# Scores of two heads at a time in the first block's attention of a fused two-block kernel

## The chip, the cores and the metric

The kernel runs on one core of one Trainium2 chip. The metric is the device time of one execution in microseconds, the median of the runs. The core has five engines with a queue of instructions each: TensorE (PE in the profile), VectorE (DVE), ScalarE (ACT), GpSimd (POOL) and SyncE (SP, which issues the transfers). Each takes its queue in order, and they wait for each other through semaphores.

## What is computed

Two transformer-like blocks are applied to 256 tokens of width 1024. The change is in the first block's attention, which has three kinds with eight heads each, 64 wide: `slc` (causal over selected blocks; with 256 tokens and 64-token blocks all of them are selected), `win` (a causal window) and `dsa` (each query sees the 64 keys that an indexer scores highest). Cut to what matters:

```python
# per kind and head; tq = query position, kpos = key position
s = jnp.einsum('bqd,bkd->bqk', q, k) * HEAD_DIM ** -0.5
p = masked_softmax(s, mask)          # mask: kpos <= tq; for dsa also "among the top 64"
o = jnp.einsum('bqk,bkd->bqd', p, v)
# slc and win: head h uses key/value group h // 4; dsa: one key and value for all heads
```

Beside it `mod = c @ w_ada + b_ada` is needed, a row of 6144 numbers from a 1024 x 6144 matrix.

## The kernel before, in words

All of it is one program with a hand-written order on every engine. The weights come through a ring of four 1 MB tiles in SBUF, loaded by SyncE in a fixed order.

The attention of the first block is a loop over 24 units, `UNITS1` (L243): `slc` heads 0 to 7, `win` heads 0 to 7, `dsa` heads 0 to 7. I call the steps of unit i as follows, with the line that the profile gives:

- S(i), PE, `scores` (L752, matmuls by the helper at L659): for each of the two blocks of 128 queries one fp32 matmul of the query (64 x 128) with the keys (64 x 128, then 64 x 256), and behind each a bf16 matmul of an identity (128 x 128) with the mask, which adds the mask in PSUM. Queries and keys of a head lie on half of the partitions: of group `h // 4` (`slc`, `win`) or `h % 2` (`dsa`). The result is 128 x 384 in PSUM bank i % 2.
- M(i), DVE, L2013: two row maxima of that bank.
- E(i), ACT, L1349: two exponentials out of the bank into `prob`, with row sums. Its end frees the bank.
- T(i), PE, `turn` (L764, matmuls at L768): three 128 x 128 transposes of `prob` into bank 2 + i % 2.
- C(i), DVE, L2021: the copy of that bank to SBUF.
- V(i), PE, `values` (L772, L659 again): three fp32 matmuls (128 x 128 with 128 x 64) into the banks of the kind's output.

PE's queue holds in turn S(i), T(i-1), V(i-2) (L789 to L795). DVE's queue (`attention` at L2004) holds in turn M(i), C(i-1) and then `after1(i - 2)` (L2034), which carries work from beside the attention:

- K, `key_round` (L1960, L1967 to L1976): one of 16 rounds that find the top 64 keys for `dsa`, 8 for each block of queries. The last of a block writes the mask `maskd`, which S of the first `dsa` unit waits for.
- W, `weigh` (L1819, L1829 and L1831): one of 16 tiles of `w_ada`, four DVE instructions of 128 x 512 that add up columns times `c`. It stands in every second step up to unit 13 and in every step after that.
- O, `weighted` and `coefficients` (L1978, L1993): twice, for `slc` and for `win`, the output of a finished kind is scaled and added.

The PSUM banks are planned by `attention_groups` (L247). Behind the attention PE runs `modulation(1)` (L738), 64 matmuls with one moving column, and then the output projection.

Of the kernel before, what the change touches and what calls it, by code (L numbers as in the profile page):

```python
# [28 lines left out]
TB = T // P  # L29
# [3 lines left out]
HEADS = 8  # L33
# [10 lines left out]
DSA_K = min(256, T // 4)  # L44
# [195 lines left out]

UNITS1 = [(kind, h) for kind in ("slc", "win", "dsa") for h in range(HEADS)]  # L243
O_BANK = {"slc": 4, "win": 6, "dsa": 4}


def attention_groups(group, units):  # L247
    n = len(units)
    for i in range(n + 2):
        if i < n:  # L250
            group(("S", *units[i]), i % 2)
        if 1 <= i <= n:
            group(("PT", *units[i - 1]), 2 + (i - 1) % 2)
        if i >= 2 and units[i - 2][1] == 0:
            for tb in range(TB):
                group(("O", units[i - 2][0], tb), O_BANK[units[i - 2][0]] + tb)


IN2_KIND = ["mq"] + [name for name in ("hgf", "hgq", "sbq", "sbk", "hig", "sbv") for _ in range(2)]
# [21 lines left out]
def build(nc, x_in, mem_in, pos_in, vec_in, ident_in, const_in, w_in, out):  # L281
    with ExitStack() as ctx:
# [60 lines left out]
        identb = take(P // 2).bitcast(BF16)  # L343
# [295 lines left out]
        def _(pe):  # L639
            order = iter(PLAN)  # L640

            def begin(name):

                assert next(order) == name, name
                bank, use = PLAN[name]
                if use > 1:
                    pe.wait_ge(drained[bank], use - 1)
                return banks[bank]

            def end(ins, name):  # L650
                ins.then_inc(full[PLAN[name][0]], 1)
# [4 lines left out]
                    pe.wait_ge(loaded[n % RING], 16 * (n // RING + 1))  # L656

            def mm(out_, lhsT, rhs, start=True, stop=True):
                return nc.tensor.matmul(out_, lhsT, rhs, start=start, stop=stop)  # L659

            def both_halves(ps, cols, head):

# [85 lines left out]
            def attention(units, operands, v_of, cols, mask):  # L748

                n = len(units)  # L750

                def scores(i):  # L752
                    ps = begin(("S", *units[i]))
                    for tb in range(TB):
                        q, k = operands(units[i], tb)
                        a, b = cols[tb]
                        m = mask(units[i], tb)
                        last = mm(ps[:, a:b], q, k, stop=(m is None))
                        if m is not None:
                            lo, mat = m  # L760
                            last = mm(ps[:, a + lo:b], identb, mat, start=False)
                    end(last, ("S", *units[i]))

                def turn(i):  # L764
                    wait_read(pe, ("S", *units[i]))
                    ps = begin(("PT", *units[i]))
                    for c in range(cols[1][1] // P):
                        last = nc.tensor.transpose(ps[:, c * P:(c + 1) * P],  # L768
                                                   prob[:, i % 2, c * P:(c + 1) * P], ident[:, :])
                    end(last, ("PT", *units[i]))  # L770

                def values(i):  # L772
                    kind, h = units[i]
                    if h == 0:
                        for tb in range(TB):
                            begin(("O", kind, tb))
                    wait_read(pe, ("PT", kind, h))
                    for tb in range(TB):
                        ps = banks[PLAN[("O", kind, tb)][0]]
                        a, b = cols[tb]  # L780
                        for c in range(a // P, b // P):
                            last = mm(ps[:, h * HD:(h + 1) * HD], probT[:, i % 2, c * P:(c + 1) * P],
                                      v_of(units[i], c - a // P), start=(c == a // P), stop=(c == b // P - 1))
                        if i + 1 == n or units[i + 1][0] != kind:
                            end(last, ("O", kind, tb))
                    pe.drain().then_inc(s_pvd, 1)

                base = 0 if units is UNITS1 else len(UNITS1)
                for i in range(n + 2):  # L789
                    if i < n:  # L790
                        scores(i)
                    if 1 <= i <= n:
                        turn(i - 1)
                    if i >= 2:
                        values(i - 2)  # L795


            pe.wait_ge(s_small, SMALL)
# [5 lines left out]
            out_ = [begin(("mkv", tb)) for tb in range(TB)]  # L804
            for half in range(2):
                arrived(("mem_kv", 0, half))
                for tb in range(TB):
                    for kk in range(4):
                        k = 4 * half + kk
                        last = mm(out_[tb][:, :], hT[:, k, tokens(tb)], km(("mem_kv", 0, half))[:, kk, :],  # L810
                                  start=(k == 0), stop=(k == KD - 1))
# [9 lines left out]
            ps = begin(("mkT",))  # L821
            for pr in range(2):
                for tb in range(TB):
                    last = nc.tensor.transpose(ps[:, pr * T + tb * P:pr * T + (tb + 1) * P],
                                               mkv[:, tb, pr * P:(pr + 1) * P], ident[:, :])
            end(last, ("mkT",))
            pe.wait_ge(s_rot, 1)
            for n in range(7):
                ps = begin(("pairT", n))
                for s in range(2):  # L830
                    pair = 2 * n + s
                    for tb in range(TB):
                        cols = slice(s * T + tb * P, s * T + (tb + 1) * P)
                        if pair < PAIR_KD:
                            first = 2 * pair if pair < PAIR_KS else 2 * pair + 2
                            last = nc.tensor.transpose(ps[:, cols], rot[:, tb, first * HD:(first + 2) * HD],
                                                       ident[:, :])
                        else:
                            r = ROT_KD if pair == PAIR_KD else ROT_KI
                            last = both_halves(ps, cols, rot[:, tb, r * HD:(r + 1) * HD])  # L840
# [3 lines left out]
            for which, src, first in (("kcT", rot, ROT_KC * HD), ("vcT", plain, PL_VC)):  # L844
                ps = begin((which,))
                for g in range(2):
                    for tb in range(TB):
                        a = first + g * HD
                        last = both_halves(ps, slice(g * T + tb * P, g * T + (tb + 1) * P), src[:, tb, a:a + HD])
                end(last, (which,))  # L850
            for which in range(2):
# [3 lines left out]
                ps = begin(("cmp", which))  # L855
                for m in range(16):
                    last = mm(ps[:, 0:45], w1[:, m, :], kvT[which][:, :, 2 * m:2 * m + 225:16],
                              start=(m == 0), stop=(m == 15))
# [3 lines left out]
            ps = begin(("kcmp",))  # L862
            for g in range(2):
                last = mm(ps[g * HD:(g + 1) * HD, 0:N_CMP], vall("w2k"), hidk[:, g, 0:N_CMP])
            end(last, ("kcmp",))
            wait_read(pe, ("cmp", 1))
            ps = begin(("vblk",))
# [5 lines left out]
            for g in range(2):  # L873
                ps = begin(("Sc", g))
                rows = slice(g * HD, (g + 1) * HD)
                for tb in range(TB):
                    for r in range(4):
                        c = (tb * 4 + r) * 16
                        last = mm(ps[:, c:c + N_CMP], pairT[rows, PAIR_QN + r, tokens(tb)], kcmpT[rows, 0:N_CMP])
                end(last, ("Sc", g))  # L880

            for n in range(4):
                tb, odd = n // 2, n % 2
                width = (tb + 1) * P
                ps = begin(("L", n))
                rows = slice(odd * HD, (odd + 1) * HD)
                for i in range(2):
                    last = mm(ps[:, i * width:(i + 1) * width], pairT[rows, PAIR_QI + i, tokens(tb)],
                              pairT[rows, PAIR_KI, 0:width])
                end(last, ("L", n))  # L890
            pe.wait_ge(s_pcz, 1)
            ps = begin(("pcT",))
            for tb in range(TB):
                last = nc.tensor.transpose(ps[:, tb * P:(tb + 1) * P],
                                           sc[:, tb * HEADS:(tb + 1) * HEADS, :].rearrange("p h n -> p (h n)"),
                                           ident[:, :])
# [3 lines left out]
            for tb in range(TB):  # L900
                ps = begin(("Oc", tb))
# [32 lines left out]
            for n in range(4):  # L934
                ps = begin(("gg", n))
                for k in range(4):
                    last = mm(ps[:, k * P:(k + 1) * P],
                              gg[:, 4 * n + k:4 * n + k + 1].to_broadcast([P, P]), ident[:, :])
# [5 lines left out]
            out_ = {}  # L944
# [766 lines left out]
        def _(dve):  # L1711
# [248 lines left out]
            def key_round(i):  # L1960


                tb, r = i // 8, i % 8
                width = (tb + 1) * P
                s, w = score[:, tb, 0:width], work[:, tb, 0:width]
                if r == 0:
                    link(tt(score[:, tb, tb * P:width], score[:, tb, tb * P:width], con("causal"), ALU.add))  # L1967
                src = s if r == 0 else w
                link(nc.vector.max(cmax[:, 0:8], src))
                link(nc.vector.match_replace(w, cmax[:, 0:8], src, TAKEN))  # L1970
                if r == DSA_K // 8 - 1:

                    link(ts(w, w, 0.5 * TAKEN, NEG, ALU.is_ge, ALU.mult))
                    if tb:
                        nc.vector.tensor_copy(maskd[:, tb, 0:P], w[:, 0:P])
                    tt(maskd[:, tb, tb * P:width], w[:, tb * P:width], con("causal"), ALU.add).then_inc(s_maskd, 1)  # L1976
# [56 lines left out]

            def after1(i):  # L2034

                if 0 <= i + 2 < TB * DSA_K // 8:
                    key_round(i + 2)
                if i + 2 >= 16 or i % 2 == 0:
                    if rest:
                        weigh(rest.pop(0))  # L2040
                if i in (8, 16):
                    kind = UNITS1[i - 1][0]
                    coefficients(kind, 1 if kind == "slc" else 2)
                    for tb in range(TB):
                        weighted(kind, ("O", kind, tb), tb, 0, True)
# [472 lines left out]
```

## Time and profile before

| | us |
|---|---|
| median of 3 runs | 1652.7 |
| lowest and highest run | 1650.15, 1653.73 |
| time of the profiled execution | 1652.53 |
| its span in the trace | 1650.7 |
| PE busy, PEld (weight loads) busy | 1497.5, 1307.3 |
| DVE busy | 968.1 |
| ACT busy | 725.8 |
| POOL busy | 1005.4 |

PE's busy time is modelled where matmuls overlap, so 91% busy isn't 91% used. The table is a sum over stages that differ; the attention above is 107 us of the span, and the page's row of PE's clock shows which of the two levels (half or full) was granted in each slice. The chain of work that ended last, cut to a stretch, tells there which engine the others waited for; gaps in an engine's own line tell what it waited for.

### The profile page before, as it was taken

How to read it: one execution, taken by the hardware profiler on the slowest of the kernel's cores; microseconds unless marked ns; L12 is line 12 of the kernel's file. 1: busy time of each engine (PE TensorE's matmuls, PEld its weight loads, DVE VectorE, ACT ScalarE, POOL GpSimd, SP SyncE). 2: the span in 40 equal slices, each digit the busy share in tenths (PEclk: the TensorE clock that was granted, in tenths of full speed). 3: DMA queues.
4: the chain of work that ended last, by engine and by line, in shares of the span. 5: the costliest groups of instructions: out<-in, count | busy, mean ns of one | idle time of the engine just before them, and what ended most of it. 6: DMA issues, size and time to landing. Idle time of an engine off the chain costs nothing.

```text
span 1650.7 us, 24575 instructions
## 1 busy us (share of the span) xinstructions
PE 1497.5 (91%) x9944; PEld 1307.3 (79%) x9944; DVE 968.1 (59%) x1618; ACT 725.8 (44%) x1292; POOL 1005.4 (61%) x729
## 2 busy tenths in 40 slices
PE   0699899969999599979998989999999999999998
PEld 0378567759987588658998989999998878888886
DVE  4463788255511586452586583877768999952221
ACT  2234211355644566434444545334343444445554
POOL 0162000337676354135699899666667878889997
PEclk9998555789999799989999999999999999999999
DMA  6444235225555232124544445433433443445552
GB/s 264 171 153 154 77 128 204 76 78 179 179 179 185 96 128 103 52 76 149 187 175 169 167 169 187 137 145 132 151 129 130 151 150 134 152 172 185 200 183 102
DMA packets 34481, 244.99 MB, mean 148 GB/s; under 512 B 3904, under 2 KB 4288, under 8 KB 5184
## 3 DMA queue, kind: packets, MB, share of 16 engines
q1 hardware_dynamic: 33376, 241.19, 41.0%
q10 hardware_dynamic: 992, 2.23, 0.4%
q8 instruction: 79, 1.29, 0.3%
q14 instruction: 34, 0.28, 0.0%
HBM read 242.36 MB, written 1.05 MB: 147 GB/s over the span
## 4 chain that ended last, share of the span: by engine, by line
PE 76%; DVE 12%; ACT 3%; POOL 3%; issue 2%; PEld 2%; DMA 1%; PEldq 0%; ACTq 0%; DVEq 0%
PE bank L659 34%; PE bank L1236 20%; PE bank L691 20%; POOL v_lo L1706 2%; PEld bank L691 2%; DVE ada L1831 2%; PE bank L1020 1%; DMA arena<-pos_dram 1%; DVE arena L1831 1%; DVE hot L2375 1%; ACT arena L1294 1%; POOL v_lo L1696 1%; DVE arena L2256 1%; DVE x L1798 1%; PE bank L768 0%
## 5 line engine op out<-in xcount | busy, mean ns | idle before, releaser
L1706 POOL TENSOR_TENSOR v_lo<-ring,v_hi 128x512 fp32r<-128x512 f32 x512 | 712.5, 1407 | 136.0 <-ACT v_hi L1650 120.5
L1696 POOL TENSOR_TENSOR v_lo<-ring,d_hi 128x512 fp32r<-128x512 f32 x213 | 292.8, 1384 | 499.8 <-ACT d_hi L1336 436.0
L1650 ACT CAST v_hi<-ring 128x512 fp32r<-128x512 f32 x512 | 317.9, 622 | 452.5 <-PE bank L659 238.7
L659 PE MATMUL bank<-hT_hi,v_hi 128*128 128x256 f32 x1024 | 293.2, 286 | 8.7 <-POOL v_lo L1706 8.7
L659 PE MATMUL bank<-hT_lo,v_hi 128*128 128x256 f32 x1024 | 288.3, 282 | 0.0
L659 PE MATMUL bank<-hT_hi,v_lo 128*128 128x256 f32 x1024 | 286.9, 280 | 0.0
L1336 ACT CAST d_hi<-ring 128x512 fp32r<-128x512 f32 x236 | 143.5, 620 | 174.9 <-PE bank L691 140.1
L1236 PE MATMUL bank<-v_hi,mix_hi 128*128 128x512 f32 x512 | 206.9, 404 | 0.4 <-DVE mix_lo L2392 0.4
L659 PEld LDWEIGHTS bank<-hT_hi,v_hi 128*128 128x128 f32 x1024 | 194.6, 190 | 10.1 <-POOL v_lo L1706 8.2
L1236 PE MATMUL bank<-v_hi,mix_lo 128*128 128x512 f32 x512 | 201.0, 392 | 0.0
L1236 PE MATMUL bank<-v_lo,mix_hi 128*128 128x512 f32 x512 | 199.8, 390 | 0.0
L659 PEld LDWEIGHTS bank<-hT_lo,v_hi 128*128 128x128 f32 x1024 | 193.3, 189 | 0.0
L659 PEld LDWEIGHTS bank<-hT_hi,v_lo 128*128 128x128 f32 x1024 | 192.4, 188 | 0.0
L1781 DVE TENSOR_TENSOR v_lo<-ring,d_hi 128x512 fp32r<-128x512 f32 x71 | 62.8, 885 | 219.0 <-ACT d_hi L1336 210.8
L2392 DVE TENSOR_TENSOR mix_lo<-arena,mix_hi 128x512 fp32r<-128x512 f32 x64 | 86.7, 1355 | 133.0 <-ACT mix_hi L1662 133.0
L659 PE MATMUL bank<-arena 128*128 128x128 f32 (+7 forms) x600 | 145.1, 391 | 13.2 <-DVE arena L2185 3.1
L691 PE MATMUL bank<-hT_hi,d_hi 128*128 128x256 f32 x528 | 149.3, 283 | 5.9 <-issue 2.9
L691 PE MATMUL bank<-hT_lo,d_hi 128*128 128x256 f32 x528 | 148.5, 281 | 0.0
L691 PE MATMUL bank<-hT_hi,v_lo 128*128 128x256 f32 x528 | 147.7, 280 | 0.0
L659 PEld LDWEIGHTS bank<-arena 128*128 128x128 f32 (+3 forms) x600 | 105.8, 250 | 48.9 <-issue 35.6
L659 PE MATMUL bank<-hotg,hot 128*128 128x64 bf16 x1536 | 116.8, 241 | 4.0 <-DVE mix_lo L2392 2.6
L659 PEld LDWEIGHTS bank<-hotg,hot 128*128 128x128 bf16 x1536 | 94.0, 119 | 25.0 <-issue 11.8
(308 smaller groups left out, 2547.8 us busy)
## 6 DMA issues: line engine op xcount, KB each, us to landing
ring<-w_dram SPq DMA_DIRECT2D x228, 1024.0 KB, 4.8
arena<-mem_dram ACTq DMA_DIRECT2D x1, 1024.0 KB, 8.4
x<-x_dram SPq DMA_DIRECT2D x1, 1024.0 KB, 7.5
out_dram<-x SPq DMA_DIRECT2D x1, 1024.0 KB, 4.0
arena<-const_dram ACTq DMA_DIRECT2D x1, 884.0 KB, 18.4
arena<-vec_dram ACTq DMA_DIRECT2D x1, 144.0 KB, 15.3
ident<-ident_dram ACTq DMA_DIRECT2D x1, 64.0 KB, 10.6
iota<-ident_dram ACTq DMA_DIRECT2D x1, 64.0 KB, 12.8
```

What stands on the lines that cost most here:

```text
L659: return nc.tensor.matmul(out_, lhsT, rhs, start=start, stop=stop)
L691: last = nc.tensor.matmul(out_, l, m, start=start and part == 0, stop=stop and part == 2, skip_group_check=True)
L1020: return nc.tensor.matmul(out_, lhsT, rhs, start=start, stop=stop, skip_group_check=True)
L1236: last = nc.tensor.matmul(acc[tb, c][:, :], w[:, q % 2, t], v[:, r, :], start=False, stop=(q == PAIRS - 1 and jj == 1 and part == 2), skip ...
L1294: link(nc.scalar.activation(junk, src[:, tb, :], ACT.Square, accum_out=ssq[:, 2 * i + tb:2 * i + tb + 1]))
L1336: nc.scalar.copy(d_hi[:, r, :], dense_quarter(d, r)).then_inc(s_dhi, 1)
L1650: nc.scalar.copy(v_hi[:, r, :], quarter(at, r)).then_inc(s_vhi, 1)
L1696: nc.gpsimd.tensor_tensor(v_lo[:, r, :], dense_quarter(d, r), d_hi[:, r, :], ALU.subtract).then_inc(s_dpl, 1)
L1706: nc.gpsimd.tensor_tensor(v_lo[:, r, :], quarter(at, r), v_hi[:, r, :], ALU.subtract).then_inc(s_plo if r < 3 else w_used, 1)
L1781: tt(v_lo[:, 3, :], dense_quarter(d, 3), d_hi[:, 3, :], ALU.subtract).then_inc(s_dvl, 1)
L1831: ins = stt(acc, w, vcol("c", k), acc, ALU.mult, ALU.add)
L2392: tt(mix_lo[:, q % 2, :], pair_weights(q), mix_hi[:, q % 2, :], ALU.subtract).then_inc(s_mlo, 1)
```

## The change

The units are put in the order of heads 0, 4, 1, 5, 2, 6, 3, 7 for `slc` and `win`, so that two neighbours lie on different halves of the partitions; `dsa` heads have that already. PE takes two units in a step: S of both units, with the four mask matmuls first and then the score matmuls of the two heads in turn; then T, V, T, V. Before the pair of S it waits until both banks are free. DVE's and ACT's loops stay, but for the key rounds, which come one step earlier.

```diff
-UNITS1 = [(kind, h) for kind in ("slc", "win", "dsa") for h in range(HEADS)]
+PAIRED = {"slc": (0, 4, 1, 5, 2, 6, 3, 7), "win": (0, 4, 1, 5, 2, 6, 3, 7), "dsa": range(HEADS)}
+UNITS1 = [(kind, h) for kind in ("slc", "win", "dsa") for h in PAIRED[kind]]
...
             def mm(out_, lhsT, rhs, start=True, stop=True):
-                return nc.tensor.matmul(out_, lhsT, rhs, start=start, stop=stop)
+                return nc.tensor.matmul(out_, lhsT, rhs, start=start, stop=stop, skip_group_check=True)
...
                 def scores(i):
-                    ps = begin(("S", *units[i]))
+                    two = [begin(("S", *units[i + j])) for j in range(2)]
                     for tb in range(TB):
-                        q, k = operands(units[i], tb)
                         a, b = cols[tb]
-                        m = mask(units[i], tb)
-                        last = mm(ps[:, a:b], q, k, stop=(m is None))
-                        if m is not None:
-                            lo, mat = m
-                            last = mm(ps[:, a + lo:b], identb, mat, start=False)
-                    end(last, ("S", *units[i]))
+                        m = [mask(units[i + j], tb) for j in range(2)]
+                        for j in range(2):
+                            lo, mat = m[j]
+                            mm(two[j][:, a + lo:b], identb, mat, start=(tb == 0), stop=False)
+                    for tb in range(TB):
+                        a, b = cols[tb]
+                        for j in range(2):
+                            q, k = operands(units[i + j], tb)
+                            last = mm(two[j][:, a:b], q, k, start=False, stop=True)
+                            if tb == TB - 1:
+                                end(last, ("S", *units[i + j]))
...
-                for i in range(n + 2):
+                for i in range(0, n + 4, 2):
                     if i < n:
                         scores(i)
-                    if 1 <= i <= n:
-                        turn(i - 1)
-                    if i >= 2:
-                        values(i - 2)
+                    for j in (i - 2, i - 1):
+                        if 0 <= j < n:
+                            turn(j)
+                        if 0 <= j - 1 < n:
+                            values(j - 1)
...
             def after1(i):
 
-                if 0 <= i + 2 < TB * DSA_K // 8:
-                    key_round(i + 2)
+                if i + 2 == 0:
+                    key_round(0)
+                if i + 3 < TB * DSA_K // 8:
+                    key_round(i + 3)
```

`attention_groups` (the plan of the banks) follows PE's new order, with the same banks.

On PE, in the middle of the `slc` units, there stood before (bank0 and bank1 hold scores, bank2 and bank3 transposes, bank4 and bank5 outputs; "drained" is the semaphore that a bank's reader raises) V, S of one unit and the T of the unit before it:

```order
L659 MATMUL bank4<-arena 128x64 [waits bank3_drained]
L659 MATMUL bank5<-arena 128x64 x2
L659 MATMUL bank0<-arena 128x128 [waits bank0_drained]
L659 MATMUL bank0<-arena 128x128
L659 MATMUL bank0<-arena 128x256
L659 MATMUL bank0<-arena 128x128
L768 MATMUL bank3<-ident,arena 128x128 [waits bank3_drained,bank1_drained]
L768 MATMUL bank3<-ident,arena 128x128 x2
```

and now the same place reads:

```order
L666 MATMUL bank0<-arena 128x128 [waits bank1_drained,bank0_drained]
L666 MATMUL bank1<-arena 128x128
L666 MATMUL bank0<-arena 128x128
L666 MATMUL bank1<-arena 128x128
L666 MATMUL bank0<-arena 128x128
L666 MATMUL bank1<-arena 128x128
L666 MATMUL bank0<-arena 128x256
L666 MATMUL bank1<-arena 128x256
L779 MATMUL bank2<-ident,arena 128x128 [waits bank2_drained,bank0_drained]
L779 MATMUL bank2<-ident,arena 128x128 x2
L666 MATMUL bank4<-arena 128x64 [waits bank3_drained]
L666 MATMUL bank5<-arena 128x64 x2
```

The first transpose of the older pair (into bank2) now stands behind the scores of the younger pair, and these wait for both score banks.

On DVE the place of the loop is this, now, in the `dsa` units (the maxima of an odd unit, the copy of the even unit before it, W, the maxima and the copy of the next step, W):

```order
L2024 TENSOR_REDUCE stat<-bank 128x1 [waits bank1_drained,bank1_full,w_used]
L2024 TENSOR_REDUCE stat<-bank 128x1
L2032 COPY arena<-bank 128x384 [waits unit_done,bank2_full]
L1842 SCALAR_TENSOR_TENSOR arena<-ring,arena 128x512 [waits slot3_loaded]
L1842 SCALAR_TENSOR_TENSOR arena<-ring,arena 128x512 [waits vector_step] x3
L2024 TENSOR_REDUCE stat<-bank 128x1 [waits bank0_drained,bank0_full,w_used]
L2024 TENSOR_REDUCE stat<-bank 128x1
L2032 COPY arena<-bank 128x384 [waits unit_done,bank3_full]
```

This order of maxima, copy and W is the one of before; nothing stands between the maxima of the odd unit (bank1) and the copy from bank2.

## Rows read from the trace of the kernel before

**Rows 1.** Page, the span in 40 slices of 41.3 us, tenths
```profile
PE   0699899969999599979998989999999999999998
DVE  4463788255511586452586583877768999952221
PEclk9998555789999799989999999999999999999999
```
**Rows 2.** Busy time by stretch: PE, PEld, DVE, ACT, POOL, then granted clock, DMA
```profile
178.00:216.00 38.00, 35.39 (x129) 25.17 (x129) 30.80 (x80) 8.21 (x36) 0.00 (x0) 0.53 0.31 111
216.00:256.00 40.00, 36.28 (x126) 25.55 (x125) 33.28 (x76) 8.22 (x36) 0.00 (x0) 0.50 0.37 132
256.00:285.00 29.00, 26.40 (x97) 19.82 (x96) 27.35 (x50) 5.48 (x24) 0.00 (x0) 0.50 0.62 218
```
**Rows 3.** Chain that ended last, slc units: start us, us, what
```profile
188.74 0.64 PE bank L768 x3
189.38 1.17 PE bank L659 x6
190.55 0.08 issue
190.63 2.38 PE bank L659 x6
193.01 0.64 PE bank L768 x3
```
**Rows 4.** The same chain, dsa units and behind the attention
```profile
268.24 0.41 DVE stat L2013
268.65 0.46 DVE arena L2021
...
272.12 0.41 DVE stat L2013
...
284.69 1.54 PE bank L659 x6
286.24 0.26 issue
286.49 13.80 PE bank L659 x64
```
**Rows 5.** Groups of DVE, 178 to 285 us: busy, mean ns, idle before
```profile
L2021 DVE COPY arena<-bank 128x384 f32<-128x384 f32 x24 | 13.3, 552 | 0.4 <-PE bank L768 0.3
L2013 DVE TENSOR_REDUCE stat<-bank 128x1 f32<-128x128 f32 x24 | 7.0, 292 | 12.4 <-issue 7.2 <-PE bank L659 4.7
```
**Rows 6.** Timeline of all engines, 171 to 200 us
```profile
178.06 0.62 DVE L2013 TENSOR_REDUCE stat<-bank 128x1 f32<-128x128 f32 x2 [1.01 <-PE bank L659]
...
183.95 0.20 ACT L1349 ACTIVATION_READ_ACCUMULATOR arena<-bank,stat 128x1 f32 x1
...
184.20 0.90 PE L768 MATMUL bank<-ident,arena 128*128 128x128 f32 x3 [1.59 <-ACT arena L1349]
...
185.14 0.56 DVE L2021 COPY arena<-bank 128x384 f32<-128x384 f32 x1 [0.29 <-PE bank L768]
...
193.10 0.62 DVE L2013 TENSOR_REDUCE stat<-bank 128x1 f32<-128x128 f32 x2 [1.95 <-issue]
...
193.81 0.37 ACT L1349 ACTIVATE arena<-bank,stat 128x128 f32<-128x128 f32 x1 [2.71 <-PE bank L659]
...
194.52 0.20 ACT L1349 ACTIVATION_READ_ACCUMULATOR arena<-bank,stat 128x1 f32 x1
```
**Rows 7.** Timeline of PE's weight loads inside one S, then T
```profile
190.62 0.50 PEld L659 LDWEIGHTS bank<-arena 64*128 64x128 f32 x2 [0.26 <-issue]
191.35 0.72 PEld L659 LDWEIGHTS bank<-arena 128*128 128x128 bf16 x3 [0.22 <-issue]
192.72 0.10 PEld L659 LDWEIGHTS bank<-arena 128*128 128x128 bf16 x1 [0.65 <-issue]
```
**Rows 8.** Indexer scores: timeline of PE; matmuls of L659 at 165.70 to 165.80
```profile
164.04 3.16 PE L659 MATMUL bank<-arena 64*128 64x128 f32 x15
L659 PE MATMUL bank<-arena x4: 631/631/631, 165.3 to 165.7; 64*128 64x256 f32 x4
```

More of the change, by code:

```diff
@@ L248, in attention_groups, with first @@
     n = len(units)
-    for i in range(n + 2):
-        if i < n:
-            group(("S", *units[i]), i % 2)
-        if 1 <= i <= n:
[L253 to L256, printed above, removed]
+    def first(i):
+        if 0 <= i < n and units[i][1] == 0:
+            for tb in range(TB):
+                group(("O", units[i][0], tb), O_BANK[units[i][0]] + tb)
+    for i in range(0, n + 4, 2):
+        if i < n:
+            group(("S", *units[i]), 0)
+            group(("S", *units[i + 1]), 1)
+        for j in (i - 2, i - 1):
+            if 0 <= j < n:
+                group(("PT", *units[j]), 2 + j % 2)
+            first(j - 1)
 IN2_KIND = ["mq"] + [name for name in ("hgf", "hgq", "sbq", "sbk", "hig", "sbv") for _ in range(2)]
@@ L752, in scores @@
                 def scores(i):
-                    ps = begin(("S", *units[i]))
+                    two = [begin(("S", *units[i + j])) for j in range(2)]
                     for tb in range(TB):
-                        q, k = operands(units[i], tb)
                         a, b = cols[tb]
-                        m = mask(units[i], tb)
-                        last = mm(ps[:, a:b], q, k, stop=(m is None))
-                        if m is not None:
-                            lo, mat = m
-                            last = mm(ps[:, a + lo:b], identb, mat, start=False)
-                    end(last, ("S", *units[i]))
+                        m = [mask(units[i + j], tb) for j in range(2)]
+                        for j in range(2):
+                            lo, mat = m[j]
+                            mm(two[j][:, a + lo:b], identb, mat, start=(tb == 0), stop=False)
+                    for tb in range(TB):
+                        a, b = cols[tb]
[4 more added lines that the diff above has]
+                                end(last, ("S", *units[i + j]))
                 def turn(i):
@@ L786, in values @@
                     pe.drain().then_inc(s_pvd, 1)
-                base = 0 if units is UNITS1 else len(UNITS1)
-                for i in range(n + 2):
+                for i in range(0, n + 4, 2):
                     if i < n:
                         scores(i)
-                    if 1 <= i <= n:
-                        turn(i - 1)
-                    if i >= 2:
-                        values(i - 2)
+                    for j in (i - 2, i - 1):
+                        if 0 <= j < n:
+                            turn(j)
+                        if 0 <= j - 1 < n:
+                            values(j - 1)
             pe.wait_ge(s_small, SMALL)
```

## The prediction

> **What bounds the kernel now.** I began with the page's slices [rows 1]: PE is nearly full everywhere, but in slices 4 to 6 (165 to 289 us), where the attention lies, the granted clock is 5 tenths, the 1.2 GHz level. So this stage runs at half speed although PE looks busy. The busy time by stretch [rows 2] splits it by kind: in the `slc` units DVE is busy 30.8 of 38 us, in the `win` units 33.3 of 40, in the `dsa` units 27.4 of 29, and PE 35.4, 36.3 and 26.4. Two engines are close to each other, so the chain must say which one the others wait for. In the `slc` units it runs on PE alone [rows 3]: T 0.64, V 1.17, issue 0.08, S 2.38, a period of 4.27 us (188.74 to 193.01). In the `dsa` units it runs on DVE [rows 4]: maxima, copy, W, 3.88 us from 268.24 to 272.12; with the other form of W 4.14. The `win` units lie between. Behind the last V stand 13.80 us of one-column matmuls on PE [rows 4], which nothing in the change touches.
>
> What DVE loses in the whole stage stands before its maxima and copies: 7.2 + 4.7 + 0.3 = 12.2 us [rows 5], of which the first 1.0 comes before the first unit [rows 6]. So **11.2 us are DVE's waits inside the stage**, out of the 106.6 from the first maxima (178.06) to the last copy (284.6); the other 95.4 are work that it does one piece after the other and that the change only reorders. No version in which DVE does the same work can gain more than those 11.2 us.
>
> **The change, part by part.**
>
> *Scores.* Today one S is 0.08 + 2.38 = 2.46 us. In it are four score passes (each fp32 matmul of L659 is two), of 128, 128, 256 and 256 columns, and two masks. A pass of 128 columns costs 0.21 us where nothing disturbs it (T is three in 0.64 [rows 3]), so four passes would be 6 x 0.213 = 1.28 us and two masks at most as much as two transposes, 0.43. The rest, some 0.75 us or more, is lost at the changes between 64 rows and 128 rows: from the first score load to the first mask load 0.73 us pass (190.62 to 191.35) for two passes worth 0.43 [rows 7], and there are four such changes in a unit. The new pair has two in all.
>
> Do the two halves run side by side? The trace has such a case: the indexer's scores, whose last two groups lie on different halves. 15 passes, eight of 256 and six of 128 columns and a short one, take 3.16 us from the first start to the modelled end of the last [rows 8]; end to end they would need 22 x 0.213 = 4.7. And four matmuls of 256 columns, 0.43 us each, start between 165.3 and 165.7 [rows 8]. So they overlap. For the pair I have 0.45 for four masks (a mask's load is 0.10 us [rows 7]; between 0.10 and 0.21 each), 0.3 for two changes, 1.35 for the scores (1.28 if wholly side by side, 2.56 if not at all) and 0.1 for the first load: **2.2 us for two units instead of 4.9**. The bounds are 2.0 and, if nothing at all is won, 4.9.
>
> The overlap works across the order of issue here, since matmuls of the second half start before the last of the first half. The Trainium skill, "TensorE: Matmul & The Clock Gate", section "The mechanism", says otherwise: matmuls start and end strictly in the order of the program, and only weight loads of another row group are pulled ahead. This is the third rival below.
>
> *PE's demand* falls by that from 8.54 to 2 x (0.64 + 1.17) + 2.2 = 5.8 us for a pair. PE isn't the bound any more in any kind. If that were all, DVE would bound the stage.
>
> *The order of the waits.* It isn't all. The pair of S waits for both score banks, so for E of both units of the pair before, and T of the even unit stands behind it on PE. DVE's queue has M(i+1), C(i) with nothing between, and C(i) needs T(i). So after M(i+1), i even, DVE stands still while the whole chain runs: from the end of the maxima to E 0.09 (193.10 + 0.62 to 193.81), E 0.91 (to 194.52 + 0.20), to PE 0.05 (184.15 to 184.20), the pair of S 2.2, and from the start of T to C 0.94 (184.20 to 185.14) [rows 6]. **Together 4.19 us, once for each pair.** None of it is hidden: K, W and the next maxima are all queued behind C(i) on DVE, and ACT and PE have nothing left of the older pair. Before, C(i-1) needed T(i-1), for which PE had waited only for E(i-1); its scores in front needed E of two units back. DVE hardly waited for T: 0.3 us in 24 copies [rows 5].
>
> Eleven of the twelve pairs are followed by another pair and pay it: 11 x 4.19 = 46.1 us. The waits of before, 11.2 us, go away, since with 5.8 us of work in a period of 10 to 12 PE never makes DVE wait elsewhere; a few small ones stay (C(15), whose transposes come late behind the first `dsa` pair, 0.8, and some tenths at C(3) and C(5)), which I put at 1.2. The first maxima come 0.5 later, because four masks and four score matmuls precede them. On the other side of a pair nothing is late: the second T is ready about when DVE has done C(i), K and M(i+2), 0.46 + 0.6 to 0.95 + 0.54 against V and T, 1.8.
>
> *Key rounds.* The same 16, one step earlier; two stand before the first W, which delays M(1) by 0.6 but takes it away later: nothing. It is needed, since S of the first `dsa` pair is now in front of T(14).
>
> *The rest.* SP, POOL and ACT have the same instructions. W takes its tiles more slowly, so the ring is less pressed than now (218 GB/s in the `dsa` units [rows 2]). The 13.80 us and all behind them only move. ACT's waits lengthen and cost nothing of themselves.
>
> *Sum*: 46.1 - 11.2 + 1.2 + 0.5 = +36.6. On the profiled execution, 1652.5 (0.2 under the median of the runs), that is **1689.1 us**.
>
> **Check by periods.** A `dsa` pair takes 3.88 + 4.14 = 8.0 us now and 12.2 then, three times (the last pair has no such wait); a `slc` pair 8.5 now, and then two maxima and copies 2.0, two K 1.2, W 3.0 and the wait 4.2, together 10.4; a `win` pair with longer K (0.95 each) 11.1 against about 8. This gives 3 x 4.2 + 4 x 1.9 + 4 x 3.1 = 33 and the 0.5 of the start. It is 3 us less than the sum, since some W and O cover waits of before twice; the range takes it in.
>
> **The rivals.**
>
> 1. *The wait is hidden, faster.* It decides at C(i): if DVE's new wait there is under 11.2 / 11 = 1.0 us a pair, the change gains. This would need T(i) before the pair of S, or work between M(i+1) and C(i) on DVE; the orders printed for both engines show neither. For it speaks only that PE's demand falls by 2.7 us a pair. With no wait at all it gives 1652.5 - 11.2 = 1641. Chance 0.04.
> 2. *The change doesn't do what it says: the halves don't overlap.* Then the scores of a pair are 2.56 instead of 1.35, 1.2 us more in each of 11 waits: 1702. Against it are the four starts of [rows 8]. That fp32 passes alternate two and two, and that the pair's stationary operands change each time, is for it. Chance 0.11.
> 3. *Starts in order of issue.* The passes are issued two for one head, then two for the other. If none may start before the one ahead of it, the second head's first pass runs beside the first head's second, and then each waits for its own half: 1.28 grows to about 1.7, 0.4 us more: 1693. [Rows 8] speak against it, as four passes on only two halves lie in 0.4 us, but they are modelled in part. By that rule of "TensorE: Matmul & The Clock Gate" the trace shouldn't show them so. Chance 0.20.
> 4. *The clock rises.* Denser scores might bring 2.4 GHz into the stage. S and T of each wait would halve, 1.4 us in 11 waits, and the one-column matmuls 6.9: 1667, still slower. Against it: at 178 to 216 PE was 93% busy and got 0.53 [rows 2], and it will have more gaps. Chance 0.04.
>
> **How the numbers follow.** The forecast, a wait of 4.2 us on DVE in eleven pairs with the halves side by side, has 0.56; rivals 0.04, 0.11, 0.20, 0.04; 0.05 for what I haven't thought of. The likeliest is 1689. For the range: S of a pair at its lower bound of 2.0 gives 1687, and the small parts of the wait (0.09, 0.05, 0.94) may shrink by half where PE's loads go ahead, 0.5 us each time, 1681; I go to 1680. On the other side 1702 is rival 2 and the low part of the bound up to 4.9 (2.7 x 11, 1719); I go to 1703, which leaves out rivals 1 and 4 and half of rival 2. Under 0.2% (3.3 us) a measurement of this kernel can't tell a change from none. Faster by more is rival 1, 0.04; the same 0.02; slower 0.94.
>
> **What would show it.** In the changed kernel: the copy's group (now L2032) with some 46 us of idle before it, released by the transposes; about 11 gaps of 4.2 us; the maxima's idle down to 1 or 2 us; PE's busy share in the stage down to two thirds; the clock at 0.5 up to the end of the one-column matmuls, which start at about 323 in place of 286.5. The chain would alternate DVE, ACT, PE in each pair. S of a pair from first to last start 2.2 us: 2.6 is rival 3, 3.4 rival 2. Copies without waits of 4 us would make the prediction wrong, whatever the time.

## The result, and the profile after

| | us |
|---|---|
| before, median of 4 runs | 1652.3 (1650.15 to 1653.73) |
| changed, median of 4 runs | 1689.4 (1688.44 to 1690.63) |
| ratio, 95% interval | 1.0226 (1.0208 to 1.0244) |
| span of the changed kernel's trace | 1686.7 |

The kernel became slower by 37 us, at the forecast of 1689. First the busy time by stretch of the changed kernel, over the attention; the columns are those of [rows 2].

```profile
178.00:222.00 44.00, 20.64 (x102) 15.90 (x101) 25.00 (x65) 7.30 (x32) 0.00 (x0) 0.54 0.27 96
222.00:270.00 48.00, 22.62 (x110) 18.54 (x109) 31.54 (x74) 7.30 (x32) 0.00 (x0) 0.50 0.21 73
270.00:322.00 52.00, 27.14 (x132) 21.78 (x131) 33.71 (x62) 7.30 (x32) 0.00 (x0) 0.53 0.41 146
```

PE's first column was 35.4, 36.3 and 26.4 us in [rows 2]; now it is 20.6, 22.6 and 27.1 of longer stretches. DVE's share fell too. Over these 144 us PE is busy for 70 and DVE for 90, so each stands still for a good part of the time: that is a chain of waits. The chain that ended last shows one pair, from the end of its maxima on (start us, us, what):

```profile
206.23 0.92 ACT arena L1360 x4
207.15 0.14 issue
207.29 2.17 PE bank L666 x12
209.46 0.83 PE bank L779 x3
```

E 0.92, the pair of S 2.17 and T 0.83 follow each other, where [rows 3] had PE alone. The timeline has the start of T and DVE's copies, with the idle time in front of each copy and what ended it:

```profile
209.39 0.90 PE L779 MATMUL bank<-ident,arena 128*128 128x128 f32 x3
210.32 0.56 DVE L2032 COPY arena<-bank 128x384 f32<-128x384 f32 x1 [4.18 <-PE bank L779]
212.60 0.56 DVE L2032 COPY arena<-bank 128x384 f32<-128x384 f32 x1 [0.47 <-PE bank L779]
...
272.66 0.56 DVE L2032 COPY arena<-bank 128x384 f32<-128x384 f32 x1 [4.35 <-PE bank L779]
274.94 0.56 DVE L2032 COPY arena<-bank 128x384 f32<-128x384 f32 x1 [1.19 <-PE bank L779]
283.30 0.56 DVE L2032 COPY arena<-bank 128x384 f32<-128x384 f32 x1 [4.39 <-PE bank L779]
```

There are eleven gaps of over 4 us, seven of 4.18 or 4.19 and four of 4.35 to 4.40. The groups of DVE from 178 to 322 us answer to [rows 5] (the last copy lies behind it):

```profile
L2032 DVE COPY arena<-bank 128x384 f32<-128x384 f32 x23 | 12.8, 554 | 49.6 <-PE bank L779 49.6
L2024 DVE TENSOR_REDUCE stat<-bank 128x1 f32<-128x128 f32 x24 | 7.0, 291 | 1.9 <-PE bank L666 1.2
```

The copies' idle time went from 0.4 to 49.6 us, the maxima's from 12.4 to 1.9 (of which 1.15 stand before the first maxima, as 1.01 did before). Last, the end of the stage:

```profile
321.77 0.76 DVE arena L1842
...
323.35 0.57 DVE arena L2032
...
325.76 13.79 PE bank L666 x64
```

The one-column matmuls begin at 325.76 instead of 286.49 [rows 4] and still take 13.8 us.

**Some of the loss is not in the total.** The stage ends 39.3 us later (325.76 - 286.49), but the span grew by 36.0. Nothing was changed in the work behind the stage, yet it takes 3.3 us less. Most of that lies in one stretch; its busy time, before and then after:

```profile
594.00:878.00 284.00, 259.89 (x1809) 231.04 (x1807) 171.94 (x354) 142.75 (x243) 149.86 (x106) 0.96 0.35 123
```
```profile
634.00:914.00 280.00, 257.71 (x1810) 228.58 (x1809) 172.06 (x354) 143.08 (x244) 149.70 (x106) 0.98 0.35 125
```

The same PE instructions (1809, give or take one) took 4 us less, at a mean granted clock of 0.98 instead of 0.96. It isn't a matter of when this work starts. From the first one-column matmul to the end of the span the ten traces of this document take between 1360.5 and 1364.3 us: the kernel before 1364.2 with a start at 286.5, the changed kernel 1360.9 with a start at 325.8, the last one below 1360.6 with a start at 287.8. So these 3.3 us are spread and no part of the mechanism; what sets them is not shown.

### The profile page after: what moved, and what is told of

It reads as the page before. It is cut to its first block, busy times and chain, and to the rows that moved or that the text cites. A ratio compares the mean times of both kernels' runs of the same rounds, so it can differ in the third digit from the quotient of the medians.

```text
span 1686.7 us, 24584 instructions
## 1 busy us (share of the span) xinstructions
PE 1469.6 (87%) x9944; PEld 1292.8 (77%) x9944; DVE 964.6 (57%) x1618; ACT 725.8 (43%) x1292; POOL 1008.8 (60%) x729
## 3 DMA queue, kind: packets, MB, share of 16 engines
HBM read 242.36 MB, written 1.05 MB: 144 GB/s over the span
## 4 chain that ended last, share of the span: by engine, by line
PE 74%; DVE 12%; issue 5%; ACT 3%; POOL 3%; PEld 2%; DMA 1%; PEldq 0%; ACTq 0%; DVEq 0%
PE bank L666 32%; PE bank L698 20%; PE bank L1247 19%; POOL v_lo L1717 2%; PEld bank L698 1%; DVE ada L1842 1%; PE bank L1031 1%; DMA arena<-pos_dram 1%; DVE arena L1842 1%; DVE hot L2388 1%; PE bank L779 1%; ACT arena L1360 1%; ACT arena L1305 1%; DVE arena L2269 1%; POOL v_lo L1707 1%
## 5 line engine op out<-in xcount | busy, mean ns | idle before, releaser
L666 PE MATMUL bank<-hT_lo,v_hi 128*128 128x256 f32 x1024 | 287.8, 281 | 0.0
L666 PE MATMUL bank<-hT_hi,v_lo 128*128 128x256 f32 x1024 | 286.5, 280 | 0.0
L666 PE MATMUL bank<-arena 128*128 128x128 f32 (+7 forms) x600 | 113.2, 383 | 77.9 <-ACT arena L1360 67.4
L666 PEld LDWEIGHTS bank<-arena 128*128 128x128 f32 (+3 forms) x600 | 90.8, 251 | 92.0 <-issue 82.3
L1247 PEld LDWEIGHTS bank<-v_hi,mix_lo 128*128 128x128 f32 x512 | 96.1, 188 | 22.1
```

The lines of the kernel that those rows point to most:

```text
L1247: last = nc.tensor.matmul(acc[tb, c][:, :], w[:, q % 2, t], v[:, r, :], start=False, stop=(q == PAIRS - 1 and jj == 1 and part == 2), skip ...
```

## The experiments

All were compared with the kernel before, run beside them on the same chip; its median was 1651.4 us beside the first four (10 runs) and 1651.0 beside the last four (19 runs).

### W in front of the copy

VectorE's queue is changed, PE's isn't: `weigh` moves to odd steps, between the maxima and the copy.

```diff
                         ins.then_inc(s_nmax, 1)
+                    if i % 2 == 1 and i < len(units):
+                        weigh1(i - 2)
                     if 1 <= i <= len(units):
...
+            def weigh1(i):
+                if (i + 2 >= 16 or i % 2 == 1) and rest:
+                    weigh(rest.pop(0))
...
-                if i + 2 >= 16 or i % 2 == 0:
-                    if rest:
-                        weigh(rest.pop(0))
+                if not (i % 2 == 1 and i + 2 < len(UNITS1)):
+                    weigh1(i)
```

> The changed kernel with one thing moved on VectorE: in odd steps the modulation tile (W, four instructions, 2.84 to 3.12 us) stands between the maxima M(i+1) and the copy C(i); W of the first two kinds is moved from even to odd steps for it. PE is as in the changed kernel. Theory 'VectorE idles at C(i) while exp, pair of S and T run': W covers 3.0 of each 4.2 us wait, 11 x 1.2 = 13 us of waits stay, so 1652.5 - 11.2 + 13 + 2 = about 1656 (1653 to 1661), idle before the copies down from 49.6 to about 13 us. Rival 'PE itself is slower with pairs, since it waits for two banks at once': the order on VectorE doesn't matter, 1689.

Measured: 1658.2 us (1654.3 to 1659.0, 7 runs), ratio 1.0032 (1.0016 to 1.0048). The copy's group, from 178 to 320 us:

```profile
L2034 DVE COPY arena<-bank 128x384 f32<-128x384 f32 x24 | 13.3, 556 | 19.4 <-PE bank L779 19.3
```

31 of the 37 us come back from the order of one queue that runs no part of the scores. What now fills the wait is the same work as before, in another place. The idle time left is 19.4 rather than 13 us: 1.2 to 1.5 in each first copy, as expected, and up to 1.2 in the second copies, whose T stands behind V on PE, which I hadn't counted.

### The control: W in odd steps, behind the copy

```diff
-                if i + 2 >= 16 or i % 2 == 0:
+                if i + 2 >= 16 or i % 2 == 1:
```

> Control for the kernel with W as cover: W of the first two kinds moved from even to odd steps, but behind the copy C(i), not in front of it. Theory of the idle copy: nothing is covered, 1688 to 1690, idle before the copies again about 50 us. Rival 'W was merely badly placed in even steps': most of the loss goes, about 1657.

Measured: 1686.0 us (1684.2 to 1687.1), ratio 1.0204 (1.0187 to 1.0222). The same group:

```profile
L2032 DVE COPY arena<-bank 128x384 f32<-128x384 f32 x24 | 13.2, 552 | 46.8 <-PE bank L779 46.8
```

So it isn't the odd step that helped but the place in front of the copy. The kernel came out 3.4 us faster than the changed one and 2 us below the range that I expected; 2.8 us less idle time before the copies goes with it.

### T and V in front of the pair of S

Now only PE's order (and the banks' plan with it):

```diff
-                    if i < n:
-                        scores(i)
                     for j in (i - 2, i - 1):
                         if 0 <= j < n:
                             turn(j)
                         if 0 <= j - 1 < n:
                             values(j - 1)
+                        if j == i - 2 and i < n:
+                            scores(i)
```

> Only PE's order is changed: T and V of the older pair's first unit stand in front of the pair of S (T(i), V(i-1), S(i+2, i+3), T(i+1), V(i)). VectorE as in the changed kernel. Theory: C(i) no longer waits; the wait moves to the maxima M(i+2), which need exp of i+1 (0.09 + 0.91 + 0.05), S 2.2 and some 0.4, 3.6 us from the end of M(i+1), of which the copy 0.47 and a key round 0.62 to 0.95 are covered: 2.2 to 2.5 us in 8 pairs, nothing in the last kind where W covers it. 1652.5 - 11.2 + 19 + 1 = 1661 (1656 to 1666), idle before the copies under 5 us, before the maxima about 20. Rival 'PE is slower with pairs': 1689.

Measured: 1659.1 us (1657.4 to 1660.3), ratio 1.0042 (1.0025 to 1.0059). Groups of DVE, 178 to 320 us:

```profile
L2032 DVE COPY arena<-bank 128x384 f32<-128x384 f32 x24 | 13.2, 552 | 1.8 <-PE bank L779 1.7
...
L2024 DVE TENSOR_REDUCE stat<-bank 128x1 f32<-128x128 f32 x24 | 7.0, 291 | 20.1 <-issue 12.7 <-PE bank L666 6.6
```

The wait moved from the copies to the maxima, at the size expected (about 20 us). The wait is thus a matter of what stands in front of the first T on PE. Two orders make it, PE's and VectorE's, and a change to either takes away most of it.

### Both: the fastest version

The last edit together with the control's: W in odd steps, behind the copy, so that it stands in front of the maxima that now wait.

> PE's order as in the kernel with T and V in front of S, and W of the first two kinds in odd steps, so behind C(i) and in front of M(i+2) everywhere. Theory: W (3.0 us) and the copy cover the 3.6 us; almost no wait on VectorE is left: 1652.5 - 11.2 + 1 to 3 = 1642 to 1644, faster than both kernels, and VectorE's work bounds the stage. Rival 'overlapping halves win nothing that VectorE can use': 1652 or more.

Measured: **1639.7 us** (1636.9 to 1642.7), ratio 0.9922 (0.9906 to 0.9939): 11.6 us faster than before, 50 faster than the change as made. Groups of DVE from 178 to 320 us, and the stretch from 178 to 276 us:

```profile
L2032 DVE COPY arena<-bank 128x384 f32<-128x384 f32 x24 | 13.2, 551 | 1.3 <-PE bank L779 1.2
...
L2024 DVE TENSOR_REDUCE stat<-bank 128x1 f32<-128x128 f32 x24 | 7.0, 291 | 2.0 <-PE bank L666 1.0
```
```profile
178.00:276.00 98.00, 72.37 (x348) 58.16 (x348) 91.23 (x203) 21.95 (x96) 0.00 (x0) 0.53 0.46 163
```

DVE is busy 91.2 of 98 us. Of the other 6.8, 1.0 stand before the first maxima and 1.7 in ten gaps of 0.08 to 0.28 us; the rest is mostly the 0.02 to 0.04 us between linked instructions. In the trace the stage ends 9.9 us earlier than before (276.60 and 286.49), near the bound of 11.2 us which the prediction set. The W in odd steps cost nothing here and won 19 us against the kernel with PE's order alone, though by itself (the control) it won 3.

### The same half in each pair

```diff
-PAIRED = {"slc": (0, 4, 1, 5, 2, 6, 3, 7), "win": (0, 4, 1, 5, 2, 6, 3, 7), "dsa": range(HEADS)}
+PAIRED = {"slc": range(HEADS), "win": range(HEADS), "dsa": (0, 2, 4, 6, 1, 3, 5, 7)}
```

> The changed kernel with pairs whose two heads lie on the same half of the partitions (slc and win heads 0,1 | 2,3 and so on, dsa heads 0,2 | 4,6 | 1,3 | 5,7); everything else is as changed. Theory 'the halves run side by side': the four passes of the second head no longer hide, 1.28 us in each of 11 waits, pair of S 3.4 to 3.5 instead of 2.17, 1689.4 + 14 = 1703 (1700 to 1707). Rival 'the shorter S comes from the masks in front, not from the halves': 1689.

Measured: 1701.8 us (1699.5 to 1701.9), ratio 1.0296 (1.0265 to 1.0327). The pair of S in its chain:

```profile
208.90 3.44 PE bank L666 x12
212.34 0.83 PE bank L779 x3
```

3.44 against 2.17 us: 1.27 more, the four passes of one head (1.28 in the prediction), to 0.01. The idle time before the copies grew from 49.6 to 63.6 us, 14.0 for 11 waits of 1.27; the time as a whole grew by 12.4. So the halves overlap fully in the change.

### Head by head instead of alternating

```diff
-                    for tb in range(TB):
-                        a, b = cols[tb]
-                        for j in range(2):
+                    for j in range(2):
+                        for tb in range(TB):
+                            a, b = cols[tb]
                             q, k = operands(units[i + j], tb)
                             last = mm(two[j][:, a:b], q, k, start=False, stop=True)
-                            if tb == TB - 1:
-                                end(last, ("S", *units[i + j]))
+                        end(last, ("S", *units[i + j]))
```

> The changed kernel without the alternation: both score matmuls of the first head, then both of the second, which lie on different halves; masks in front as changed. Theory 'a half starts as soon as it is free, whatever was issued in front for the other half', as the indexer's scores seem to show: pair of S still about 2.2 us, 1689. Rival 'matmuls start in the order of issue': the second head's passes start beside the first head's last pass of 256 columns, 1.28 + 0.85 instead of 1.28, pair of S 3.0 us, 11 x 0.85 = 9 us more, 1698.

Measured: 1689.4 us (1687.4 to 1690.6), ratio 1.0228 (1.0197 to 1.0259), the same as the change. Its chain:

```profile
206.72 2.17 PE bank L666 x12
208.89 0.83 PE bank L778 x3
```

The pair takes 2.17 us again. The eight weight loads of the scores, here and then in the changed kernel:

```profile
207.23 0.94 PEld L666 LDWEIGHTS bank<-arena 64*128 64x128 f32 x8 [0.20 <-issue]
```
```profile
207.80 0.93 PEld L666 LDWEIGHTS bank<-arena 64*128 64x128 f32 x8 [0.20 <-issue]
```

The single records behind these lines show the score passes starting two and two, 0.013 us apart, at 207.23, 207.61, 207.82 and 208.25 here. The alternation does nothing at this size: with four passes queued for one half, the other half's passes start beside them, though they are behind them in the program.

### Masks first alone, no pairs

```diff
...
                     for tb in range(TB):
-                        q, k = operands(units[i], tb)
                         a, b = cols[tb]
-                        m = mask(units[i], tb)
-                        last = mm(ps[:, a:b], q, k, stop=(m is None))
-                        if m is not None:
-                            lo, mat = m
-                            last = mm(ps[:, a + lo:b], identb, mat, start=False)
+                        lo, mat = mask(units[i], tb)
+                        mm(ps[:, a + lo:b], identb, mat, start=(tb == 0), stop=False)
+                    for tb in range(TB):
+                        q, k = operands(units[i], tb)
+                        a, b = cols[tb]
+                        last = mm(ps[:, a:b], q, k, start=False, stop=True)
```

The helper also passes `skip_group_check=True`, as in the change.

> The kernel before with one thing: in each single S both masks stand in front of both score matmuls; no pairs, old order of heads. Theory 'each change between 64 and 128 rows costs 0.15 to 0.3 us': two changes instead of four, S 2.46 down to 2.0 to 2.1, period of PE 4.27 down to about 3.9, of VectorE's 11.2 us of waits about half goes, 1645 to 1648. Rival 'the changes cost nothing, the passes are just slow': 1651 to 1652.

Measured: 1648.2 us (1645.5 to 1650.6, 10 runs), ratio 0.9975 (0.9960 to 0.9990). Its chain in the `slc` units:

```profile
206.61 1.97 PE bank L659 x6
208.58 0.83 PE bank L768 x3
209.41 1.17 PE bank L659 x6
```

S fell from 2.38 to 1.97, but T rose from 0.64 to 0.83. The weight loads at the end of S, before and then here, show why:

```profile
192.72 0.10 PEld L659 LDWEIGHTS bank<-arena 128*128 128x128 bf16 x1 [0.65 <-issue]
192.73 0.51 PEld L768 LDWEIGHTS bank<-ident,arena 128*128 128x128 f32 x3
```
```profile
206.93 0.93 PEld L659 LDWEIGHTS bank<-arena 64*128 64x128 f32 x4 [0.20 <-issue]
208.51 0.50 PEld L768 LDWEIGHTS bank<-ident,arena 128*128 128x128 f32 x3 [0.65 <-issue]
```

Both times 0.65 us pass between the last load for a score (64 rows) and the next load for 128 rows. Before, that was the last mask's, and T's loads followed at once (192.72 and 192.73); now it is T's own. The period is 4.06 instead of 4.27, 0.21 rather than the 0.37 that I expected. Of VectorE's waits I expected half to go (5.6 us). The maxima's idle time fell from 12.4 to 9.0 and the copies' rose from 0.4 to 1.5, so 2.2 us went, and 2.8 us of the total. This part of the change is right by itself.

### The same half in the fastest version

PE's and VectorE's order are those of the fastest version; the two heads of a pair lie on the same half.

> The fastest kernel so far (T and V in front of the pair of S, W in odd steps) with pairs on the same half. Theory: the pair of S grows by 1.28 us to 3.45, so the maxima wait 4.9 us from M(i+1), covered by copy, W and key round 4.1 to 4.4 (3.5 in dsa): 0.5 to 1.4 us more in 11 pairs, 1640 + 6 to 12 = 1646 to 1652. If the overlap of halves is worth nothing once the wait is gone: 1640.

Measured: 1649.6 us (1647.7 to 1653.8, 10 runs), ratio 0.9992 (0.9978 to 1.0007). Groups of DVE, 178 to 325 us:

```profile
L2032 DVE COPY arena<-bank 128x384 f32<-128x384 f32 x24 | 13.3, 555 | 10.0 <-PE bank L779 9.8
L2024 DVE TENSOR_REDUCE stat<-bank 128x1 f32<-128x128 f32 x24 | 7.0, 291 | 3.8 <-PE bank L666 3.2
```

The time is as expected (1646 to 1652). The waits stand before the copies (10.0) and not, as I expected, before the maxima (3.8, of which 1.05 before the first). Without the overlap the good order is not clearly faster than the kernel before; with it 11.6 us are won. So the overlap is worth some 10 us in this order.

## Why the prediction was right

**What bounds the stage**: right. The bound of 11.2 us for any version with the same DVE work was nearly reached: the fastest version won 9.9 us in the trace of the stage and 11.6 between the medians, which vary by some us.

**S of a pair, 2.2 us**: measured 2.17, and 2.38 in `dsa`, where the second masks are 256 wide; the sum had 2.2 for all. Of the terms inside, the experiments give one, the scores: 1.27 for a head's four passes (1.28), and full overlap (so the 1.35 was 0.07 too long). The masks, the changes and the first load (0.45, 0.3 and 0.1) were not measured apart.

**The wait of 4.19 us in eleven pairs**: measured 4.18 in seven and 4.35 to 4.40 in four, 46.8 us against 46.1. In the seven two pieces were off and cancel: from the end of E to the first matmul 0.14 and not 0.05, and from there to the start of T 2.10 (207.29 to 209.39) and not 2.2. From the start of T to the copy it was 0.93, as costed (0.94). The four longer ones are the `dsa` masks.

**The small terms**: mis-sized. I put 1.2 us for later copies and other waits; the second copies alone have 2.8 (1.19 at the one that I named, 0.47 twice, 0.2 several times), since T(i+1) stands behind V(i-1), and the maxima keep 0.8 behind the first one, where the sum left them none. The first maxima came 0.3 us later, not 0.5. The stage lost 39.3 us against 36.6. The total met the forecast to 0.3 us only because the unchanged work behind the stage took 3.3 us less in this trace, which is spread; that closeness is luck, the mechanism isn't.

**The check by periods** gave 33 and was worse than the sum. It took `win` at "about 8" without a row, and a `slc` pair of the changed kernel at 10.4, where the first copies of the pairs are 10.9 to 11.9 us apart.

**Key rounds, W, the ring, the one-column matmuls**: nothing, as costed. They only moved.

**The rivals.** 1, the hidden wait, needed work between M(i+1) and C(i) or T in front of S. Neither was in the change, and each, when put there, undid most of the loss (1658.2 and 1659.1 us). 2, no overlap, would have been the 1701.8 us of the same-half kernel, priced at 1702. 3, starts in the order of issue, I had given 0.20: the head-by-head kernel excludes it for queues of this length (2.17 us where I had expected 3.0 from it). The Trainium skill, "TensorE: Matmul & The Clock Gate", section "The mechanism", says that matmuls start strictly in program order; that doesn't hold here, where they go to different row halves. 4, the clock: the granted clock stayed at 0.50 to 0.54 in the stage.

## What to carry to other kernels

When work is batched on one engine, look at what now stands behind the batch in that engine's queue, and at what the other engines have queued behind its result: here two heads' scores took 2.7 us less of PE and brought a wait of 4.2 us, because the transpose that the copy needs stood behind them and VectorE had nothing between. Where a wait can't be avoided, put independent work in front of it in the queue of the engine that waits; moving W's four instructions past one copy in each pair gave back 31 of 37 us. And look for the gain of an overlap only after that: in the change it only made a wait shorter that the change itself had brought (1689.4 us against 1701.8 on the same half), in the right order it is what makes the kernel faster than before.

## What I had not expected of the hardware

That the alternation makes no difference (2.17 us both ways), and that fp32 matmuls on different row halves overlap fully: one head's four passes, 1.28 us, added nothing to the pair, and 1.27 when both heads lay on the same half. That one of the changes between 64 and 128 rows moved rather than vanished: T took 0.83 instead of 0.64 us as soon as a score and no longer a mask stood in front of it.
